# Combining attention branches: one broadcast multiply and one addition in place of four fused operations per head group

## The chip, the cores and the metric

One Trainium2 chip, one core of it. The metric is device time in microseconds (us) of one execution; each version is run several times and the median counts.

## What is computed

One decoder layer on 1024 tokens of width 1024, in float32. Attention has three families of heads side by side: 4 "nsa" heads, 8 sliding-window heads with sinks ("swa") and 4 stick-breaking heads ("sb"). Their outputs are normalised by family, concatenated and multiplied by an output matrix; a SwiGLU feed-forward block follows. The change touches the nsa family, whose output is a gated sum of three attentions over the same queries:

```python
def nsa_mixer(q, k_cmp, v_cmp, k_slc, v_slc, k_win, v_win, gate_logits, ...):
    kc, vc = nsa_compress(k_cmp, ...), nsa_compress(v_cmp, ...)
    o_cmp, o_slc = nsa_cmp_and_select(q, kc, vc, k_slc, v_slc, bias_tab)
    o_win = banded_attention(q, k_win, v_win, NSA_WINDOW, bias_tab)
    g = jax.nn.sigmoid(gate_logits)...          # one gate per token, branch and head
    return g[0] * o_cmp + g[1] * o_slc + g[2] * o_win
```

## The kernel before

The work is cut into tiles of 128 tokens, so there are 8 tiles (`n` = 0 to 7). A **job** is one kind of attention for one tile and four heads: 8 jobs "sb", 16 "swa", and then, for each tile, "win", "cmp" and "slc" of the nsa family, 24 jobs, which run in the trace from about 365 to 514 us.

A job goes through all engines. TensorE makes scores into PSUM (`scores`, lines 1042 to 1050). VectorE adds the bias and takes the row minimum (`logits`, 1452). ScalarE takes the exponential (`softmax`, 1247). TensorE transposes the weights block by block (`turn`, 1077). ScalarE or VectorE copies the block to SBUF (`keep`, lines 1277 and 1482). TensorE multiplies it with the values (`weigh`, 1097), 66 columns for each of four heads: 64 of output, and one of ones that gives the softmax denominator. All jobs accumulate in the same PSUM bank (`SUMS`, bank 7). So the first `weigh` of a job waits until the job before it is combined (`wait_combined`, semaphore `combined`).

`combine` (1491) runs on VectorE: it makes the coefficients from the denominators and the gates (two small instructions, 1505 and 1508) and applies them. For "win" and "swa" that is one multiplication of all 256 columns with the coefficients broadcast (1512). For "cmp" and "slc" it is four instructions, one for each head, that multiply 64 columns in PSUM and add them to `mix_n` in SBUF in the same pass (1518).

After "slc" the tile is normalised. ScalarE takes the squares (`squares`, 1297), VectorE scales their sum (`mean_squares`, 1524), POOL takes the root (866), VectorE multiplies (`norm_mix`, 1532), and TensorE transposes the result (`turn` of the family, 1066).

The order of instructions on each engine is not written by hand. `plan_attention` (254) is a list scheduler that runs when the kernel is built: each piece of work has an engine, a cost in ns, predecessors and an age, and the planner lets each engine take the piece that can start first, by age where several can. Its result is the order of the queues of TensorE, ScalarE, VectorE and SP (which issues the DMAs) for the whole of attention, about 125 to 519 us. Four other kinds of work are in that plan as well: `piece` (960), six products of 512 columns that are still left of the input projection and fill TensorE where nothing else is ready, up to about 365 us; `half_keep` (1178, 1364), which empties their one PSUM bank; `out_hi` and `out_lo` (1311, 1542), which split the output matrix into two parts, and `mix_hi` and `mix_lo` (1317, 1547), which do so for the first two tiles of the result; and `spread`, the DMAs (784) that lay out the queries of a group.

Behind attention lie the output product, the feed-forward block and the last normalisation (class `Finish`), which takes its roots on POOL (2652, 2656) with an exponent tile `mhalf` that it sets itself (2608).

Of the kernel before, what the change touches and what calls it, by code (L numbers as in the profile page):

```python
# [19 lines left out]
ALU = mybir.AluOpType  # L20
ACT = mybir.ActivationFunctionType

P = 128
# [230 lines left out]
def plan_attention(lay):  # L254
# [21 lines left out]
    for s in range(FIRST_PIECE, PIECES):  # L276
        h, n = s // 4, item_of(s)
        kind = T_TILES[h // 2][0]
        needs = [("cut_lo", n) if n >= FIRST_ITEMS else None]
        if s % 4 == 0 and h > FIRST_HALVES + 1:  # L280
            needs.append(("half_keep", h - 1))
        add(("piece", s), "pe", 6 * 226.5, needs, 1e4 + s)
        if s % 4 == 3 and h >= LAST_KEPT:
            add(("half_keep", h), "dve", dve(HALF), [("piece", s), ("half_scale", LAST_KEPT - 1)], -100)
        elif s % 4 == 3:
            add(("half_keep", h), "act", act(HALF), [("piece", s), ("half_lo", h - 10 if kind == "k" else 21) if h >= 20 else None], -100)
            add(("half_scale", h), "pool", 1650, [("half_keep", h)], -100)
# [19 lines left out]

    for j, job in enumerate(jobs):
# [60 lines left out]
        if job.kind == "sb":  # L369
            fresh = [("turn", lay.turn_at["sb", n - 2])] if n >= 2 else []  # L370
            add(("stick_combine", n), "act", act(256), [last] + fresh, age)
        else:
            fresh = [("turn", lay.turn_at[job.family, n - 2])] if n >= 2 else [("turn", lay.turn_at["sb", NT - 1])] if job.kind == "swa" else []
            extra = [("sink_exp", lay.j_swa[j])] if job.kind == "swa" else []
            add(("combine", m), "dve", {"swa": 900, "win": 650}.get(job.kind, 1100), [last] + fresh + extra, age)
        if job.kind in ("sb", "slc") or job.strip == 4:
            i, width = NT * FAMILIES.index(job.family) + n, FAMILY_WIDTH[job.family]
            age = 10.0 * j + 20
            add(("squares", i), "act", act(width, 250), [("stick_combine", n) if job.kind == "sb" else ("combine", m)], age)
# [86 lines left out]
def mixers(nc, core, x_rows, w_first, w_tiles, w_values, ln_pre, cmp, rel_bias, onehot, sinks, grp_g, w_out, ln_post, ln_ffn_pre, tables, keep):  # L466
# [15 lines left out]
    softmax_jobs = [j for j in range(lay.NJ) if jobs[j].kind != "sb"]  # L482
    NPHI = 8

    with ExitStack() as st:
# [96 lines left out]
        combined, stick_combined = sem("combined"), sem("stick_combined")  # L582
# [537 lines left out]
        def act_program(act, o):  # L1120
# [168 lines left out]
            def squares_(i):  # L1289
                family, n = FAMILIES[i // NT], i % NT  # L1290
                if family == "sb":
                    act.wait_ge(stick_combined, n + 1)
                else:
                    act.wait_ge(combined, 2 * n + 2 if family == "swa" else 2 * NT + 3 * n + 3)
                if i:
                    act.wait_ge(squares, i)
                act.activation(junk[:, 0:FAMILY_WIDTH[family]], mix_of(family, n), ACT.Square, accum_out=ss[:, i:i + 1]).then_inc(squares, 1)
# [27 lines left out]
        def dve_program(dve, o):  # L1325
# [165 lines left out]
            def combine(v):  # L1491
# [53 lines left out]
            def mix_lo(t):  # L1545
# [6 lines left out]
                    "combine": combine, "mean_squares": mean_squares, "norm_mix": norm_mix}  # L1552
# [78 lines left out]
def out_and_ffn(nc, core, x, x1, w_gate, w_up, w_pairs, act_pairs, keep, mem, fin):  # L1631
# [330 lines left out]
    def pool_program(pool):  # L1962
# [24 lines left out]
        fin.constants(pool)  # L1987
# [565 lines left out]
    o = {"w": w, "mH": mH, "mL": mL, "gpost": gpost, "gpre": gpre, "g_in": g_in, "wH_done": wH_done, "wL_done": wL_done,  # L2553
# [4 lines left out]
class Finish:  # L2558
# [3 lines left out]
    def __init__(self, core, stack, x1, ln_post, out, y_part, xt, gain, gained_last, junk):  # L2562
# [4 lines left out]
        self.ss, self.half, self.ms, self.rs, self.mhalf = sb("ss", [P, 2, NT]), sb("half", [P, NT]), sb("ms", [P, NT]), sb("rs", [P, NT]), sb("mhalf", [P, M_PAIRS])  # L2567
        self.x_in = [sem(f"x_in{t}") for t in range(4)]
        self.g_in, self.mhalf_set = sem("g_in"), sem("mhalf_set")
# [36 lines left out]

    def constants(self, pool):
        pool.memset(self.mhalf[:], -0.5).then_inc(self.mhalf_set, 1)
# [40 lines left out]
    def first_roots(self, pool):  # L2649
        pool.wait_ge(self.mhalf_set, 1)  # L2650
        pool.wait_ge(self.ms_done, 1)
        pool.tensor_tensor(self.rs[:, 0:M_PAIRS], self.ms[:, 0:M_PAIRS], self.mhalf[:], ALU.pow).then_inc(self.rs_done, 1)

    def root(self, pool, t):
        pool.wait_ge(self.late_ms, t - M_PAIRS + 1)
        pool.tensor_tensor(self.rs[:, t:t + 1], self.ms[:, t:t + 1], self.mhalf[:, 0:1], ALU.pow).then_inc(self.rs_done, 1)
# [28 lines left out]
def build_layer(nc, ins, out):  # L2685
# [7 lines left out]
    with ExitStack() as stack:  # L2693
# [17 lines left out]
        with ExitStack() as ffn:  # L2711
# [25 lines left out]
            with ExitStack() as early:  # L2737
# [5 lines left out]
                         (mem["xt_up"], mem["xt_sums"], mem["xt_spare"]), mem["last_gain"], mem["gained_last"], mem["last_junk"])  # L2743
# [95 lines left out]
```

## Time and profile before

| | us |
|---|---|
| median of 3 runs | 1252.41 |
| the three runs | 1250.11, 1252.41, 1258.15 |
| the profiled execution | 1252.77 |
| its span, first to last instruction | 1251.0 |
| busy: TensorE (PE) | 1217.7 |
| busy: TensorE weight loads (PEld) | 1042.2 |
| busy: VectorE (DVE) | 866.4 |
| busy: ScalarE (ACT) | 605.7 |
| busy: GpSimd (POOL) | 181.4 |

A profile tells when each instruction ran. TensorE has two rows, PE for products and PEld for the loads of the stationary operand, which overlap with them. An engine that idles is of interest only if the end of the program hangs on it. For that the profile gives the chain that ended last, and for each wait the instruction that ended it. "Granted clock" is the share of its full speed (2.4 GHz) that TensorE was given: 1.00, or 0.50 for 1.2 GHz.

### The profile page before, as it was taken

The numbers are of one execution on the slowest core, as the hardware profiler recorded it, in microseconds if no ns is written. First come the engines' busy times: TensorE is split into PE (matmuls) and PEld (weight loads), VectorE is DVE, ScalarE is ACT, GpSimd is POOL, SyncE is SP. The second block draws the span as 40 slices with busy tenths as digits, with TensorE's granted clock in tenths as the row PEclk, the third lists the DMA queues.
The fourth block names the chain that finished last, engine by engine and source line by source line (L and its number), as shares of the span: only waits on it lengthen the run. The fifth ranks groups of instructions, "written<-read, shape, count | busy, mean of one in ns | idle before, by whom it ended". The sixth has DMA issues, their size and how long they took to land.

```text
span 1251.0 us, 18763 instructions
## 1 busy us (share of the span) xinstructions
PE 1217.7 (97%) x6592; PEld 1042.2 (83%) x6592; DVE 866.4 (69%) x1641; ACT 605.7 (48%) x1167; POOL 181.4 (15%) x153
## 2 busy tenths in 40 slices
PE   9999999999999999999989999999999999999996
PEld 7898878888988999888878888888888888788885
DVE  6323788858878665355876657667666568897888
ACT  5432677657776566344653333333333345444343
POOL 5230111111000000011001112112122021000114
PEclk9999999999999999999999999999999999999998
DMA  6303511136842100222312232333332455743443
GB/s 234 120 1 119 118 37 49 35 110 158 182 121 77 26 18 18 68 101 100 119 42 100 94 125 67 103 127 103 108 105 72 144 193 195 259 156 115 151 169 135
DMA packets 66881, 136.93 MB, mean 109 GB/s; under 512 B 8503, under 2 KB 27199, under 8 KB 66788
## 3 DMA queue, kind: packets, MB, share of 16 engines
q1 hardware_dynamic: 66788, 135.74, 34.0%
q8 instruction: 53, 0.87, 0.3%
q14 instruction: 40, 0.33, 0.1%
HBM read 90.33 MB, written 28.60 MB: 95 GB/s over the span
## 4 chain that ended last, share of the span: by engine, by line
PE 79%; DVE 9%; issue 5%; ACT 3%; DMA 2%; SPq 1%; DVEq 0%; POOL 0%; ACTq 0%; POOLq 0%
PE ps L2506 32%; PE ps L2536 11%; PE ps L1097 7%; PE ps L2450 6%; PE ps L941 4%; PE ps L1077 4%; PE ps L886 3%; PE ps L960 3%; PE ps L1042 2%; PE ps L1050 2%; DVE ring L1468 2%; PE ps L975 1%; DMA m_qs<-m_qn 1%; DVE ring L1460 1%; DVE QT L2325 1%
## 5 line engine op out<-in xcount | busy, mean ns | idle before, releaser
L2506 PE MATMUL ps<-f_topH,f_W 128*128 128x512 f32 x704 | 221.0, 389 | 3.8 <-DVE f_W L2292 2.1
L2506 PEld LDWEIGHTS ps<-f_topH,f_W 128*128 128x128 f32 x704 | 132.1, 188 | 32.0 <-DVE f_W L2292 4.6
L2292 DVE TENSOR_TENSOR f_W<-f_scr,f_W 128x512 fp32r<-128x512 f32 (+1 forms) x128 | 89.9, 705 | 84.9 <-ACT f_W L2057 84.8
L2506 PE MATMUL ps<-f_topL,f_W 128*128 128x512 f32 x352 | 136.9, 389 | 0.0
L1097 PE MATMUL ps<-V,m_tw 128*128 128x66 f32 (+1 forms) x1056 | 129.2, 273 | 2.3 <-DVE m_mix_n L1518 2.2
L1097 PEld LDWEIGHTS ps<-V,m_tw 128*128 128x128 f32 x1056 | 126.3, 193 | 5.3 <-DVE m_mix_n L1518 4.3
L2536 PE MATMUL ps<-f_headH,f_W 128*128 128x512 f32 x408 | 128.0, 390 | 2.2 <-issue 1.5
L2506 PE MATMUL ps<-f_headH,f_W 128*128 128x512 f32 x352 | 114.7, 390 | 0.0
L2536 PEld LDWEIGHTS ps<-f_headH,f_W 128*128 128x128 f32 x408 | 76.6, 188 | 19.6 <-issue 2.7
L2057 ACT CAST f_W<-f_scr 128x512 fp32r<-128x512 f32 (+1 forms) x128 | 77.6, 610 | 24.6 <-PE ps L2536 15.2
L2292 DVE TENSOR_TENSOR f_W<-ring,f_W 128x512 fp32r<-128x512 f32 x60 | 59.6, 1006 | 33.4 <-ACT f_W L2057 33.3
L1277 ACT COPY m_tw<-ps 128x512 f32<-128x512 f32 (+1 forms) x101 | 56.5, 568 | 52.0 <-PE ps L1097 29.8
L2536 PE MATMUL ps<-f_headL,f_W 128*128 128x512 f32 x204 | 79.4, 389 | 0.0
L2506 PEld LDWEIGHTS ps<-f_topL,f_W 128*128 128x128 f32 x352 | 66.1, 188 | 13.7
L2506 PEld LDWEIGHTS ps<-f_headH,f_W 128*128 128x128 f32 x352 | 66.1, 188 | 13.6
L2506 PE MATMUL ps<-f_headL,f_W 128*128 128x512 f32 x176 | 68.5, 389 | 0.0
L960 PE MATMUL ps<-m_hH,m_wH 128*128 128x512 f32 x144 | 60.4, 419 | 4.9 <-ACT QT L1178 4.8
L2536 PE MATMUL ps<-f_b22H,f_W 128*128 128x512 f32 x208 | 65.1, 389 | 0.0
L2450 PE MATMUL ps<-o_w,o_mH 128*128 128x512 f32 x224 | 60.5, 392 | 0.0
L2506 PE MATMUL ps<-f_b22H,f_W 128*128 128x512 f32 x176 | 57.8, 389 | 0.0
L2325 DVE TENSOR_TENSOR QT<-ps,QT 128x512 f32<-128x512 f32 x68 | 46.7, 687 | 15.7 <-PE ps L2536 15.7
L1042 PE MATMUL ps<-m_KSa,m_qs 128*128 128x256 f32 (+7 forms) x168 | 55.0, 345 | 2.3 <-DVE m_rows_sb L1475 1.2
(279 smaller groups left out, 2660.4 us busy)
## 6 DMA issues: line engine op xcount, KB each, us to landing
act_pairs<-QT SPq DMA_DIRECT2D x77, 256.0 KB, 4.1
m_qs<-m_qn SPq DMA_DIRECT2D x128, 128.0 KB, 2.4
ring<-in_ffn_w_up SPq DMA_DIRECT2D x22, 512.0 KB, 3.7
f_stage<-act_pairs SPq DMA_DIRECT2D x40, 256.0 KB, 3.6
ring<-in_ffn_w_gate SPq DMA_DIRECT2D x19, 512.0 KB, 4.5
f_scr<-act_pairs SPq DMA_DIRECT2D x37, 256.0 KB, 3.1
ring<-in_ffn_w_down SPq DMA_DIRECT2D x11, 512.0 KB, 5.3
f_pair_up<-in_ffn_w_down SPq DMA_DIRECT2D x11, 512.0 KB, 6.6
```

What stands on the lines that cost most here:

```text
L941: ins = pe.matmul(ps[:, b + a, 0:VW_HALF], h[:, k, tok], wv[:, w, k, a * VW_HALF:(a + 1) * VW_HALF], start=(k == 0 and h is hH and w == 0) ...
L960: ins = pe.matmul(ps[:, bank, :], w[:, n % W_ITEMS, cols], a[:, k, hf * HALF:(hf + 1) * HALF], start=(k == 0 and w is wH and a is hH), sto ...
L1042: pe.matmul(out, q_hi_, k, start=True, stop=False)
L1077: ins = pe.transpose(ps[:, bank, i * P:(i + 1) * P], rows, ident[:])
L1097: ins = pe.matmul(ps[:, SUMS, wide * i:wide * (i + 1)], tw[:, t % W_SLOTS, P * i:P * i + P], v, start=(kb == 0 and i == 0), stop=(kb == jo ...
L1277: act.copy(out, src).then_inc(kept_by["act"], 1)
L2057: act.copy(slot_part(s, 0), source(s)).then_inc(hi_done, 1)
L2292: dve.tensor_tensor(slot_part(s, 1), source(s), slot_part(s, 0).bitcast(F32), ALU.subtract).then_inc(lo_done, 1)
L2325: dve.tensor_tensor(part, product_, part, ALU.add).then_inc(y_added, 1)
L2450: ins = pe.matmul(ps[:, 2 * (t % 2) + hf, :], m[:, t % 2, k, :], w[k][:, a, hf * HALF:(hf + 1) * HALF], start=(k == 0 and m is mH and a == ...
L2506: ins = pe.matmul(ps[:, bank, :], whole[:, w, cols], halves[h][:, k0 + k, col:col + HALF], start=(begins and k == 0 and w == 0 and h == 0) ...
L2536: ins = pe.matmul(ps[:, bank, :], whole[:, w, k * P:(k + 1) * P], block(n)[h], start=(begins and k == 0 and w == 0 and h == 0), stop=(k == ...
```

## The change

Three things change in the nsa family and its plan, and one at the end of the program.

1. For "cmp" and "slc", `combine` multiplies all four heads by one broadcast multiplication out of PSUM, as "win" did before, but into a spare tile in SBUF (`tmp`, 256 columns of it). `combined` is raised by that multiplication. A second step, `mix_add`, adds `tmp` to `mix_n`. It is a piece of work of its own in the plan, behind its `combine`; the next "cmp" or "slc" `combine` waits for it, as `tmp` is there once.
2. The squares of an nsa tile wait for `mix_add` of "slc" and no longer for `combined`.
3. Costs in the plan: `piece` 6 x 231 ns for 6 x 226.5; `combine` 800 ns for all kinds, before 900 (swa), 650 (win) and 1100 (cmp, slc); `mix_add` has the planner's cost of 256 columns on VectorE.
4. `Finish` uses the exponent tile that the output product's part has set already, in place of its own, whose memset goes.

```diff
-        add(("piece", s), "pe", 6 * 226.5, needs, 1e4 + s)
+        add(("piece", s), "pe", 6 * 231, needs, 1e4 + s)
...
-            add(("combine", m), "dve", {"swa": 900, "win": 650}.get(job.kind, 1100), [last] + fresh + extra, age)
+            two_step = job.kind in ("cmp", "slc")
+            added = [("mix_add", two_steps - 1)] if two_step and two_steps else []
+            add(("combine", m), "dve", 800, [last] + fresh + extra + added, age)
+            if two_step:
+                add(("mix_add", two_steps), "dve", dve(256), [("combine", m)], age + 0.5)
+                two_steps += 1
...
-                    act.wait_ge(combined, 2 * n + 2 if family == "swa" else 2 * NT + 3 * n + 3)
+                    if family == "swa":
+                        act.wait_ge(combined, 2 * n + 2)
+                    else:
+                        act.wait_ge(mix_added, 2 * n + 2)
...
                 if job.kind in ("swa", "win"):
-                    ins = dve.tensor_tensor(mix[:, job.mix_at:job.mix_at + 4 * HD].rearrange("p (h d) -> p h d", d=HD),
-                                            sums[:, :, 0:HD], coef[:, a].unsqueeze(2).broadcast_to([P, 4, HD]), ALU.mult)
+                    out = mix[:, job.mix_at:job.mix_at + 4 * HD]
                 else:
-                    dve.wait_ge(combined, v)
-                    for i in range(4):
-                        dst = mix[:, HD * i:HD * i + HD]
-                        ins = dve.scalar_tensor_tensor(out=dst, in0=sums[:, i, 0:HD], scalar=coef[:, a][:, i:i + 1], in1=dst,
-                                                       op0=ALU.mult, op1=ALU.add)
-                ins.then_inc(combined, 1)
+                    out = o["tmp"][:, 0:4 * HD]
+                    dve.wait_ge(piece_done, pieces(PIECES))
+                    if two_step_jobs.index(j):
+                        dve.wait_ge(mix_added, two_step_jobs.index(j))
+                dve.tensor_tensor(out.rearrange("p (h d) -> p h d", d=HD), sums[:, :, 0:HD],
+                                  coef[:, a].unsqueeze(2).broadcast_to([P, 4, HD]), ALU.mult).then_inc(combined, 1)
+
+            def mix_add(i):
+
+                j = two_step_jobs[i]
+                mix = mix_of("nsa", jobs[j].n)[:, 0:4 * HD]
+                dve.wait_ge(combined, j_sm[j] + 1)
+                if jobs[j].kind == "slc":
+                    dve.wait_ge(mix_added, i)
+                dve.tensor_tensor(mix, mix, o["tmp"][:, 0:4 * HD], ALU.add).then_inc(mix_added, 1)
...
-        fin.constants(pool)
...
-    def constants(self, pool):
-        pool.memset(self.mhalf[:], -0.5).then_inc(self.mhalf_set, 1)
...
-        pool.wait_ge(self.mhalf_set, 1)
```

## Rows read from the trace of the kernel before

**Rows 1.** The page of the profile: span, then busy time, share, instructions
```profile
span 1251.0 us, 18763 instructions
PE 1217.7 (97%) x6592; PEld 1042.2 (83%) x6592; DVE 866.4 (69%) x1641; ACT 605.7 (48%) x1167; POOL 181.4 (15%) x153
...
PE 79%; DVE 9%; issue 5%; ACT 3%; DMA 2%; SPq 1%; DVEq 0%; POOL 0%; ACTq 0%; POOLq 0%
```

**Rows 2.** Stretches: length, busy time (instructions) by engine, granted clock, DMA share, GB/s
```profile
140.00:290.00 150.00, 142.37 (x882) 123.65 (x881) 121.21 (x175) 105.42 (x216) 24.05 (x20) 0.99 0.25 68
290.00:365.00 75.00, 74.28 (x580) 70.38 (x579) 59.19 (x232) 49.76 (x129) 6.62 (x10) 1.00 0.62 146
365.00:405.00 40.00, 35.84 (x249) 31.96 (x248) 36.80 (x151) 31.02 (x68) 3.08 (x4) 0.96 0.36 107
405.00:510.00 105.00, 104.49 (x805) 97.25 (x804) 63.16 (x251) 59.64 (x105) 2.17 (x4) 0.98 0.09 21
```

**Rows 3.** By line: ns min/median/max, first and last start; who waited (us, times)
```profile
L1518 DVE SCALAR_TENSOR_TENSOR m_mix_n<-ps,m_coef,m_mix_n x64: 273/276/285, 372.0 to 513.9; 128x64 f32<-128x64 f32 x64
...
  PEld ps L1097: 4.3, 8
...
  PE ps L1097: 2.2, 3
...
L1512 DVE TENSOR_TENSOR m_mix_n<-ps,m_coef x8: 424/424/425, 367.5 to 499.0; 128x256 f32<-128x256 f32 x8
```

**Rows 4.** Timeline (start, us, engine, line, count), two stretches of the nsa jobs
```profile
375.87 0.97 PEld L1097 LDWEIGHTS ps<-V,m_tw 128*128 128x128 f32 x8 [0.53 <-DVE m_mix_n L1518]
...
400.54 0.86 DVE L1518 SCALAR_TENSOR_TENSOR m_mix_n<-ps,m_coef,m_mix_n 128x64 f32<-128x64 f32 x4
401.31 0.28 DVE L1452 CUSTOM_DVE_ANT_0 m_rows_slc<-ps,m_strip_full,m_neg 128x64 f32<-128x64 f32 x1
...
401.45 1.76 PEld L1097 LDWEIGHTS ps<-V,m_tw 128*128 128x128 f32 x8 [1.76 <-DVE m_mix_n L1518]
401.45 1.95 PE L1097 MATMUL ps<-V,m_tw 128*128 128x66 f32 x8 [1.52 <-DVE m_mix_n L1518]
```

**Rows 5.** Timeline, VectorE: instructions of 256 columns, each with its follower
```profile
377.77 0.42 DVE L1421 TENSOR_TENSOR m_qn<-QT,m_qn 128x256 fp32r<-128x256 f32 x1
378.10 0.48 DVE L1532 SCALAR_TENSOR_TENSOR m_mix_n<-m_mix_n,m_rs,m_g_sb 128x256 f32<-128x256 f32 x1
...
380.14 0.42 DVE L1512 TENSOR_TENSOR m_mix_n<-ps,m_coef 128x256 f32<-128x256 f32 x1
...
380.49 0.68 DVE L1482 COPY m_tw<-ps 128x512 f32<-128x512 f32 x1
```

**Rows 6.** Stretches at the low and at the full clock, columns of rows 2
```profile
401.45:408.30 6.85, 6.85 (x28) 6.85 (x29) 4.21 (x19) 4.07 (x7) 0.54 (x1) 0.50 0.50 145
230.94:234.20 3.26, 3.26 (x8) 2.59 (x9) 3.26 (x4) 0.15 (x1) 1.53 (x1) 0.50 0.00 0
...
630.00:632.00 2.00, 0.49 (x2) 0.45 (x3) 2.00 (x4) 2.00 (x5) 0.00 (x0) 1.00 0.00 0
```

**Rows 7.** Timeline, TensorE: the first products behind two other stops
```profile
230.94 0.77 PE L960 MATMUL ps<-m_hH,m_wH 128*128 128x512 f32 x1 [2.29 <-ACT QT L1178]
...
631.51 0.50 PE L2506 MATMUL ps<-f_topH,f_W 128*128 128x512 f32 x1 [2.13 <-DVE f_W L2292]
```

**Rows 8.** Timeline, 389 to 392 us: a root on POOL beside VectorE
```profile
389.45 1.22 DVE L1547 TENSOR_TENSOR o_mL<-QT,o_mH 128x1024 fp32r<-128x1024 f32 x1
389.61 1.46 POOL L866 TENSOR_TENSOR m_rs<-m_ms,m_mhalf 128x1 f32<-128x1 f32 x1 [11.83 <-DVE m_ms L1524]
...
391.80 0.41 PE L1066 MATMUL ps<-ident,m_mix_n 128*128 128x128 f32 x2 [0.27 <-DVE m_mix_n L1532]
```

**Rows 9.** By line: the memset of the last part
```profile
L2608 POOL MEMSET e_mhalf<- x1: 93/93/93, 1035.8 to 1035.8; 128x4 f32 x1
```

More of the change, by code:

```diff
@@ L306, in plan_attention @@
     add(("strip", 4), "dma", 3000, [("norm_mix", NT - 1)], -100)
+    two_steps = 0
     for j, job in enumerate(jobs):
@@ L378, in plan_attention @@
             age = 10.0 * j + 20
-            add(("squares", i), "act", act(width, 250), [("stick_combine", n) if job.kind == "sb" else ("combine", m)], age)
+            add(("squares", i), "act", act(width, 250), [("stick_combine", n) if job.kind == "sb" else ("mix_add", two_steps - 1) if job.kind == "slc" else ("combine", m)], age)
             add(("mean_squares", i), "dve", 100, [("squares", i)], age)
@@ L482, in mixers @@
     softmax_jobs = [j for j in range(lay.NJ) if jobs[j].kind != "sb"]
+    two_step_jobs = [j for j in range(lay.NJ) if jobs[j].kind in ("cmp", "slc")]
     NPHI = 8
@@ L581, in mixers @@
         kept_by = {"act": sem("turn_kept_by_act"), "dve": sem("turn_kept_by_dve")}
-        combined, stick_combined = sem("combined"), sem("stick_combined")
+        combined, stick_combined, mix_added = sem("combined"), sem("stick_combined"), sem("mix_added")
         squares, ms_ready, rs_ready, normed = sem("squares"), sem("ms_ready"), sem("rs_ready"), sem("normed")
@@ L1551, in dve_program @@
                     "stick_scan": stick_scan, "stick_sub": stick_sub, "keep": keep_turn, "sink_arg": sink_arg_,
-                    "combine": combine, "mean_squares": mean_squares, "norm_mix": norm_mix}
+                    "combine": combine, "mix_add": mix_add, "mean_squares": mean_squares, "norm_mix": norm_mix}
             for what, arg in plan["dve"]:
@@ L2551, in pe_program @@
                 product(s)
-    o = {"w": w, "mH": mH, "mL": mL, "gpost": gpost, "gpre": gpre, "g_in": g_in, "wH_done": wH_done, "wL_done": wL_done,
+    o = {"w": w, "tmp": tmp, "mH": mH, "mL": mL, "gpost": gpost, "gpre": gpre, "g_in": g_in, "wH_done": wH_done, "wL_done": wL_done,
          "mH_done": mH_done, "mL_done": mL_done, "y_done": y_done}
@@ L2558, with __init__ @@
 class Finish:
-    def __init__(self, core, stack, x1, ln_post, out, y_part, xt, gain, gained_last, junk):
+    def __init__(self, core, stack, x1, ln_post, out, y_part, xt, gain, gained_last, junk, mhalf):
         sb = lambda n, s, d=F32: core.sb("e_" + n, s, d, stack)
@@ L2566, in __init__ @@
         self.y, self.xt, self.gain, self.gained_last, self.junk = y_part, xt, gain, gained_last, junk
-        self.ss, self.half, self.ms, self.rs, self.mhalf = sb("ss", [P, 2, NT]), sb("half", [P, NT]), sb("ms", [P, NT]), sb("rs", [P, NT]), sb("mhalf", [P, M_PAIRS])
+        self.ss, self.half, self.ms, self.rs = sb("ss", [P, 2, NT]), sb("half", [P, NT]), sb("ms", [P, NT]), sb("rs", [P, NT])
         self.x_in = [sem(f"x_in{t}") for t in range(4)]
-        self.g_in, self.mhalf_set = sem("g_in"), sem("mhalf_set")
+        self.g_in, self.mhalf = sem("g_in"), mhalf
         self.squares, self.gained, self.late_gained, self.late_ms = sem("squares"), sem("gained"), sem("late_gained"), sem("late_ms")
@@ L2649, in first_roots @@
     def first_roots(self, pool):
-        pool.wait_ge(self.mhalf_set, 1)
         pool.wait_ge(self.ms_done, 1)
-        pool.tensor_tensor(self.rs[:, 0:M_PAIRS], self.ms[:, 0:M_PAIRS], self.mhalf[:], ALU.pow).then_inc(self.rs_done, 1)
+        pool.tensor_tensor(self.rs[:, 0:M_PAIRS], self.ms[:, 0:M_PAIRS], self.mhalf[:].broadcast_to([P, M_PAIRS]), ALU.pow).then_inc(self.rs_done, 1)
     def root(self, pool, t):
         pool.wait_ge(self.late_ms, t - M_PAIRS + 1)
-        pool.tensor_tensor(self.rs[:, t:t + 1], self.ms[:, t:t + 1], self.mhalf[:, 0:1], ALU.pow).then_inc(self.rs_done, 1)
+        pool.tensor_tensor(self.rs[:, t:t + 1], self.ms[:, t:t + 1], self.mhalf[:], ALU.pow).then_inc(self.rs_done, 1)
     def wait_gained(self, dve, t):
@@ L2742, in build_layer @@
             fin = Finish(core, ffn, x1, ins["ln_ffn_post"], out, keep["QT"][:].rearrange("p k (h q) -> p (k h) q", h=2),
-                         (mem["xt_up"], mem["xt_sums"], mem["xt_spare"]), mem["last_gain"], mem["gained_last"], mem["last_junk"])
+                         (mem["xt_up"], mem["xt_sums"], mem["xt_spare"]), mem["last_gain"], mem["gained_last"], mem["last_junk"], mem["mhalf"])
             o, ffn_programs = out_and_ffn(nc, core, x, x1, ins["ffn_w_gate"], ins["ffn_w_up"], ins["ffn_w_down"], act_pairs, keep, mem, fin)
```

## The prediction

> **What bounds the kernel now.** I read the page first: TensorE is busy for 1217.7 of 1251.0 us, and the chain that ended last runs on it for 79% [rows 1]. VectorE, where the change is made, is at 69%, so time taken off VectorE counts only where TensorE waits for it. The table of stretches says where that is [rows 2]. From 405 to 510 us, where nine of the sixteen changed combines run, TensorE idles 0.5 us of 105. From 365 to 405 us, where six of them run, it idles 4.2 us of 40, and VectorE is busy for 36.8: there VectorE sets the pace. From 140 to 290 us TensorE idles 7.6 us of 150, and no changed instruction lies there, only a plan made anew. Behind attention the output product and the feed-forward block are dense and bound by TensorE, so what attention saves arrives at the end whole.
>
> The waits name the place itself: weight loads of `weigh` (1097) waited 4.3 us in 8 places for the four fused operations of line 1518, and products 2.2 us in 3 of them [rows 3]. The longest is at 401.45: 1.52 us without a product [rows 4]. Behind it the granted clock is 0.50 for 6.85 us [rows 6].
>
> **The release of the sums' bank.** Before, the bank is free when the fourth fused operation ends: 276 ns each, but they overlap, and the four take 0.86 us from start to end [rows 3, 4]. After, one broadcast multiplication releases it; "win" has the same instruction with the same operands but for the place of its output, 424 ns [rows 3]. The coefficients before it do not change. The release comes 0.86 - 0.42 = 0.44 us earlier, sixteen times. That is worth nothing where TensorE has other work in its queue. The bounds: TensorE's own stops of 2.2 us are 1.52 and two that share the 0.7 left. The first gives 0.44 back and the others at most 0.7, together 1.1 us. If the weight loads set the pace (66 columns are short beside a load), the 1.76 us stop gives 0.44 and the seven others at most 4.3 - 1.76 = 2.5, together 2.9 us [rows 3, 4]. For the low end, some of it passes to the next wait, VectorE's pace. I take 1.5 us, near the lower of the two, since from 405 us on TensorE is full.
>
> **VectorE's own time.** Before, the instruction behind the four starts 401.31 - 400.54 = 0.77 us after the first [rows 4]. After: the broadcast multiplication holds the engine for 380.49 - 380.14 = 0.35 us. The addition (256 columns, both inputs and output in SBUF) is not in the trace; its nearest row is the subtraction of line 1421, which holds it for 378.10 - 377.77 = 0.33 us [rows 5]. With other work between them the pair costs 0.68. With the addition directly behind, it must wait for the multiplication's end, 0.42 + 0.33 = 0.75 and some hundredths for the semaphore. So VectorE gains 0.1 us a time or nothing: at most 0.6 us over the six in the stretch that it paces, which I count as zero. What is cut is the delay of the release, not the engine's load.
>
> The Trainium skill ("VectorE: DVE Perf Modes", section "The DRAIN you can't avoid") says that the next operation does not start until the pipeline of the one before has emptied, though one that is not held starts earlier. By its first clause the four would hold the engine for 4 x 0.276 = 1.1 us and the new pair for 0.85, a gain of 0.25 x 16 = 4 us of VectorE; the rows have 0.77, so this trace goes by the second clause and the gain is near zero.
>
> **The clock.** The stop of 1.52 us ends at half clock [rows 4, 6]. It would be 1.08 us after the change. A stop's length alone does not decide: 2.29 us at 230.94 was followed by the low clock, 2.13 us at 631.51 was not [rows 6, 7]. What differs is what went before: around 631 us the products are long and dense, from 365 to 405 us there is a row of shorter stops, and the change shortens several of them. I hold it for a little more likely than not that this fall goes. Its price: the eight loads of one weigh step take 1.76 us there and 0.97 us at full clock [rows 4], so at least 0.8 us comes back; at most it is half of 6.85, 3.4 us, if nothing but TensorE's clock set the pace. Logits on VectorE follow those scores at their own pace, so I take 2.0 us.
>
> **The later users of the sum.** The nsa squares now wait for multiplication and addition, 0.42 + 0.42 us and a semaphore, against 0.86: no change, if the addition follows at once. In the plan it is a piece of work of its own, ready 130 ns after `combine`, so VectorE may take another piece first. For "cmp" that costs nothing, nobody but VectorE waits for it. For "slc", squares, mean, root, norm_mix and TensorE's transpose stand behind it in that order. TensorE has already waited 0.27 us for a norm_mix at 391.80 [rows 8]. That is a rival below. I price it at zero in the sum, as TensorE's transpose is elsewhere queued behind other products.
>
> **The addition beside POOL.** Before, the fused operations read one tensor from PSUM; the addition reads two from SBUF. At 389.61 a root on POOL took 1.46 us beside a VectorE operation with two SBUF inputs that ran from 389.45 for 1.22 [rows 8]. POOL does little from 365 to 510 us (5.3 us busy [rows 2]), and the root of a tile comes after its own additions; a meeting costs about one addition, 0.42 us. I price it at zero, at most 8 x 0.42 = 3.4 if each root met one and nothing hid it.
>
> The Trainium skill ("SBUF — State Buffer", section "SBUF: two separate sides") says that a VectorE operation with two SBUF inputs and a GpSimd operation that reads SBUF exclude each other for a whole instruction. This speaks against the change; the 1.46 us root agrees with it. By it the sum stays within the bound just given.
>
> **The rest.** Costs in the plan are no work; they only reorder queues from about 125 us on, the DMA issues on SP too. `piece` at 231 for 226.5 moves TensorE's filler by 27 ns apiece, under 2 us over the 68 left, enough to change neighbours. This can go either way and is priced in the rivals. The memset that goes took 93 ns on POOL at 1035.8, far ahead of its user [rows 9]: zero.
>
> **The sum.** 1.5 + 2.0 = 3.5 us off the profiled execution of 1252.77 (span 1251.0 and 1.8 around it) gives 1249.3; that execution is 0.4 above the median, so 1248.9, say 1249.
>
> **The rivals.**
> 1. *Only the release counts; the low clock stays, or comes at another stop.* For it: the stop at 401.45 is still over 1 us. 1252.4 - 1.5 = 1251.
> 2. *No net gain.* TensorE waits for logits in place of the combine, since VectorE is as busy as before, or a stop of attention's first part grows by what is won. 1252.4.
> 3. *The new order helps the first part.* There 7.6 us idle and the low clock behind 230.94 (3.26 us at half, 1.6 lost [rows 6]) are at stake, 9.2 together. If half of it goes, 4.6 more than forecast: 1244.3. Against it: these stops end on ScalarE's emptying of the pieces' bank, which the change leaves alone.
> 4. *Slower: the addition comes late.* VectorE takes one long piece (1.22 us [rows 8]) between "slc" multiplication and addition, and norm_mix and TensorE's transpose shift by it. If four tiles have no slack, 4.9 us less the 1.5 won: 1255.8. It decides from two tiles on (2.4 us); at six it is 7.3 - 1.5, 1258. Against it: waits for norm_mix before are only some tenths.
>
> **How the numbers follow.** Forecast 1249: 0.36. Rival 1: 0.20. Rival 2: 0.16. Rival 3: 0.16. Rival 4: 0.12. The range, 1243 to 1256, takes in rivals 1 and 2, rival 3 at 1244.3 with a little below it, and rival 4 at 1255.8 but not its dearer form; the three runs of before lie 2.3 below to 5.7 above their median, so a median can miss its case by some 2 us. That leaves out under 0.2. One per cent is 12.5 us, about what a measurement of this kernel can tell from no change. Faster than 1239.9 needs all of the first part's 9.2 us besides the 3.5: 0.05. Slower than 1264.9 needs all eight tiles late by 1.2 us, 9.8, and more low clock on top: 0.03. Within 1%: 0.92.
>
> **What would show it.** Line 1512 with 40 instructions of 424 ns; an addition of about 420 ns, 16 times; line 1518 gone. The first weigh behind a "cmp" or "slc" starts about 0.5 us after the multiplication starts. Waits for the combine fall from 4.3 us to under 2. TensorE idles under 3 us in the nsa jobs' first 40 us, with a granted clock of 1.00. Feed-forward and end keep their lengths. The forecast is wrong if the low clock stays, if TensorE's wait for norm_mix grows beyond 1 us, or if the idle time from 140 to 290 us moves by more than 3 us.

## The result and the profile after

| | before | after |
|---|---|---|
| median of 10 runs each, us | 1251.88 (1248.59 to 1258.15) | 1257.98 (1252.98 to 1261.50) |
| span of the profiled execution | 1251.0 | 1259.7 |

The ratio is 1.0043, 95% interval 1.0022 to 1.0064. The medians lie 6.1 us apart; by the ratio the change costs 5.4 us (2.8 to 8.0). It is slower by less than the one per cent that the prediction called "within", but it went the other way than forecast (1249) and left the range (1243 to 1256) at the top.

Below, "x us by the ratio" means (ratio - 1) x 1252. Each experiment was run 5 to 12 times beside 11 to 35 runs of the kernel before on the same chip, and its ratio is to those.

The page of the kernel after (span; busy time, share, instructions; shares of the chain that ended last), against [rows 1]:

```profile
span 1259.7 us, 18737 instructions
PE 1223.8 (97%) x6592; PEld 1047.1 (83%) x6592; DVE 862.1 (68%) x1608; ACT 604.7 (48%) x1168; POOL 179.4 (14%) x152
...
PE 83%; DVE 7%; issue 4%; ACT 4%; DMA 1%; SPq 1%; POOL 0%; DVEq 0%; ACTq 0%; POOLq 0%
```

VectorE has 4.3 us less to do, TensorE is busy for 6.1 us more with the same 6592 products: part of them ran at half clock. The stretches of [rows 2], in the kernel after (columns as there):

```profile
140.00:290.00 150.00, 139.82 (x866) 121.38 (x864) 116.30 (x165) 102.58 (x208) 24.02 (x20) 0.99 0.23 63
290.00:365.00 75.00, 74.19 (x569) 69.19 (x570) 62.92 (x236) 49.37 (x134) 6.84 (x11) 1.00 0.66 156
365.00:405.00 40.00, 34.68 (x231) 31.66 (x230) 31.66 (x124) 28.94 (x65) 1.62 (x3) 0.91 0.42 118
405.00:510.00 105.00, 104.47 (x782) 95.64 (x781) 67.18 (x253) 61.66 (x113) 2.70 (x5) 0.97 0.08 21
```

TensorE idles 10.2 us of the first stretch (7.6 before), and in the third it idles 5.3 us at a granted clock of 0.91 (4.2 us at 0.96 before). VectorE has only 31.7 us of work there against 36.8: it no longer sets the pace, and TensorE still waits more.

To compare kernels whose starts differ, I cut each span at four events: the first `piece`, the last weights of "sb", the first gate coefficient of "nsa", the first output product.

| us | front | sb | swa | nsa | output and the rest | span |
|---|---|---|---|---|---|---|
| before | 119.3 | 144.8 | 102.9 | 154.3 | 729.6 | 1251.0 |
| after | 122.3 | 147.1 | 104.4 | 156.6 | 729.3 | 1259.7 |

The front is ahead of everything that the change touches and took from 118.3 to 122.4 us over seventeen profiles, without regard to the kernel, so its 3.0 us are no work of the change (the last section shows what they hang on). The other 5.7 us are three stages, 2.3 + 1.5 + 2.2, less 0.3. Only the last of the three holds a changed instruction. Each row is one execution, and that of the kernel after, 1261.50 us, is the slowest of its ten, so I read from the stages where time was lost and from the ratios how much.

The new instructions, by line (ns min/median/max, first and last start, who waited for it), against [rows 3]:

```profile
L1528 DVE TENSOR_TENSOR o_tmp<-ps,m_coef x16: 423/424/425, 378.1 to 522.2; 128x256 f32<-128x256 f32 x16
...
  PEld ps L1104: 5.2, 6
  PE ps L1104: 2.7, 1
...
L1538 DVE TENSOR_TENSOR m_mix_n<-m_mix_n,o_tmp x16: 414/419/427, 378.8 to 522.7; 128x256 f32<-128x256 f32 x16
...
  ACT m_junk L1307: 0.4, 2
```

They cost what was forecast, 424 ns and 419 ns. TensorE waits for them in fewer places, 6 for 8, but for 5.2 us where it was 4.3, and one stop of 2.7 us holds more than half. This is it, in the timeline of the kernel after:

```profile
378.13 0.42 DVE L1528 TENSOR_TENSOR o_tmp<-ps,m_coef 128x256 f32<-128x256 f32 x1
...
378.61 1.11 PE L1104 MATMUL ps<-V,m_tw 128*128 128x66 f32 x8
...
378.81 0.42 DVE L1538 TENSOR_TENSOR m_mix_n<-m_mix_n,o_tmp 128x256 f32<-128x256 f32 x1
...
380.65 0.40 ACT L1248 CAST m_qn<-QT 128x256 fp32r<-128x256 f32 x1 [1.17 <-DMA m_qs<-m_qn]
...
381.09 0.42 DVE L1431 TENSOR_TENSOR m_qn<-QT,m_qn 128x256 fp32r<-128x256 f32 x1 [1.86 <-ACT m_qn L1248]
381.43 1.22 DVE L1560 TENSOR_TENSOR o_w<-ring,o_w 128x1024 fp32r<-128x1024 f32 x1
...
382.57 0.15 DVE L1515 SCALAR_TENSOR_TENSOR m_coef<-ps,gate 128x4 f32<-128x4 f32 x1
...
382.97 0.42 DVE L1528 TENSOR_TENSOR o_tmp<-ps,m_coef 128x256 f32<-128x256 f32 x1
...
383.45 0.97 PE L1104 MATMUL ps<-V,m_tw 128*128 128x66 f32 x5 [2.67 <-DVE o_tmp L1528]
```

The first pair works as meant: multiplication at 378.13, next `weigh` 0.48 us later, addition behind it. The eight products at 378.61 are the next job's `weigh` ("slc" of tile 0) and end at 379.72, yet its coefficients start at 382.57. VectorE's queue holds two other pieces ahead of them. `query_lo` (1431) stood 1.86 us on ScalarE's `query_hi` (1248), and that on the DMAs that lay out the queries; then came `out_lo` (1560) with 1.22 us. In the order of before, this `combine` stands ahead of both. The DMAs themselves are not late. SP's queue issued them at 373.63 and before at 368.04, but the nsa stage also starts later, at 373.84 for 367.06: against its start they come 1.2 us earlier. What changed is the place of the pieces that wait for them. First after, then before (start, us of the issues, line, count):

```profile
373.63 3.09 SPq L791 DMA_DIRECT2D m_qs<-m_qn  x4
```

```profile
368.04 2.86 SPq L784 DMA_DIRECT2D m_qs<-m_qn  x4
```

Behind the stop the clock falls, and a second time near 482, with no stop over 0.3 us in the 25 us ahead of it (stretches of the kernel after, columns as in [rows 2]):

```profile
383.00:390.00 7.00, 6.55 (x26) 6.21 (x27) 5.54 (x23) 3.52 (x10) 0.54 (x1) 0.56 0.28 75
482.00:489.00 7.00, 7.00 (x37) 6.90 (x37) 2.75 (x15) 2.77 (x8) 0.00 (x0) 0.56 0.00 0
```

### The profile page after: what moved, and what is told of

Read it like the earlier page. It is cut to its first block, busy times and chain, and to the rows that moved or that the text cites. A ratio compares the mean times of both kernels' runs of the same rounds, so it can differ in the third digit from the quotient of the medians.

```text
span 1259.7 us, 18737 instructions
## 1 busy us (share of the span) xinstructions
PE 1223.8 (97%) x6592; PEld 1047.1 (83%) x6592; DVE 862.1 (68%) x1608; ACT 604.7 (48%) x1168; POOL 179.4 (14%) x152
## 4 chain that ended last, share of the span: by engine, by line
PE 83%; DVE 7%; issue 4%; ACT 4%; DMA 1%; SPq 1%; POOL 0%; DVEq 0%; ACTq 0%; POOLq 0%
PE ps L2523 32%; PE ps L2553 12%; PE ps L1104 8%; PE ps L2467 6%; PE ps L967 4%; PE ps L1084 4%; PE ps L948 4%; PE ps L893 4%; PE ps L1049 3%; PE ps L1057 2%; PE ps L982 1%; PE ps L1115 1%; DVE m_rows_sb L1485 1%; DMA m_qs<-m_qn 1%; DVE QT L2342 1%
## 5 line engine op out<-in xcount | busy, mean ns | idle before, releaser
L967 PE MATMUL ps<-m_hH,m_wL 128*128 128x512 f32 x144 | 57.4, 398 | 0.0
```

The source lines that it names most:

```text
L967: ins = pe.matmul(ps[:, bank, :], w[:, n % W_ITEMS, cols], a[:, k, hf * HALF:(hf + 1) * HALF], start=(k == 0 and w is wH and a is hH), sto ...
```

## The experiments

**The instructions or the order.** The change has two halves that can be had apart: what VectorE executes, and the plan's inputs, which give every engine another order. The planner's code, run for both kernels, gives queues of the same 596 pieces of work on TensorE, of which at least 105 have to be moved to turn one order into the other; of SP's 52 it is 6. On ScalarE and VectorE 41 copies (`keep`) also change the engine. Kernel e1 has the new instructions in exactly the old order, with the addition directly behind its multiplication; e2 has the four fused instructions in the new order.

```diff
# e1, against the kernel after
-        add(("piece", s), "pe", 6 * 231, needs, 1e4 + s)
+        add(("piece", s), "pe", 6 * 226.5, needs, 1e4 + s)
-            add(("combine", m), "dve", 800, [last] + fresh + extra + added, age)
+            add(("combine", m), "dve", {"swa": 900, "win": 650}.get(job.kind, 1100), [last] + fresh + extra, age)
...  (the addition's piece goes, and the squares follow `combine`)
                                   coef[:, a].unsqueeze(2).broadcast_to([P, 4, HD]), ALU.mult).then_inc(combined, 1)
+                if job.kind in ("cmp", "slc"):
+                    mix_add(two_step_jobs.index(j))
# e2, against the kernel after: combine() and the squares' wait are those of before, and
...
             def mix_add(i):
+                pass
```

> The two new instructions in the order that the kernel before has on every engine (the addition directly behind its multiplication, all costs in the plan as before). Theory O (the loss is the new order, the new instructions gain a little): 1249 to 1252, ratio to before 0.997 to 1.000, stops of TensorE and the clock from 140 to 365 us as in before. Rival I (the new instructions themselves cost: the wait between multiplication and addition, or POOL beside the addition): 1255 to 1258, ratio 1.003 to 1.005, with longer waits for the combine in the nsa jobs.

> The four fused operations in the new order of every engine (the addition's place in the plan does nothing). Theory O: 1257 to 1260, as the changed kernel or a little above it, ratio to before 1.004 to 1.007. Rival I: 1250 to 1253, ratio 0.999 to 1.001.

| | median us | ratio (95%) | by the ratio |
|---|---|---|---|
| e1 new instructions, old order | 1251.56 | 0.9995 (0.9984 to 1.0006) | -0.6 |
| e2 old instructions, new order | 1262.08 | 1.0079 (1.0064 to 1.0095) | +9.9 |

Theory O of the expectations says that the order costs it, rival I that the new instructions do. The loss is the order's: e1 came as O expected, and e2 even above its 1257 to 1260. With the old instructions the new order costs 9.9 us; the new ones take back some 4.5 of them (e2 to after; the two intervals together leave about 3 either way). In the old order they give 0.6 with zero inside the interval. The stop of [rows 4] at 401.45 (1.52 us, then half clock) looks like this in e1:

```profile
403.88 1.11 PE L1100 MATMUL ps<-V,m_tw 128*128 128x66 f32 x8 [1.24 <-DVE o_tmp L1524]
```

shorter by 0.28 us, and eight products take 1.11 us where they took 1.95: full clock. The nsa stage took 152.0 us against 154.3. The 2.67 us stop of the new order stands in e2 as well, with the old instructions, at 2.97 us:

```profile
382.98 1.34 PE L1104 MATMUL ps<-V,m_tw 128*128 128x66 f32 x5 [2.97 <-DVE m_mix_n L1528]
```

**Which of the costs.** Three edits feed the planner: `piece` 226.5 to 231, `combine` to 800 for all kinds, and the addition as a piece of work of its own.

```diff
# e3: before, with 6 * 231 for piece        # e8: before, with 800 for every combine
# e4: after, with 6 * 226.5 for piece       # e7: after, with all old costs; the addition keeps its piece
# e12: e7, with 800 for "cmp" and "slc" alone
```

> The kernel before with one number changed: 231 for 226.5 ns in the planned cost of a piece. Theory O splits here. If the pieces' new order is the larger part (the changed kernel's stretch up to the last stick-breaking row was 2.3 us longer in its profile), 1254 to 1256, ratio 1.002 to 1.004. If the order behind it is (combine costs, the addition as work of its own), 1252, ratio 0.999 to 1.001. Rival I: 1252.

> The changed kernel with the planned cost of a piece put back to 226.5 ns. Counterpart of the run before: if the pieces' order is the larger part, 1253 to 1255, ratio to before 1.001 to 1.003; if the rest of the plan is, 1257 to 1258, ratio 1.004 to 1.005. Rival I: 1257 to 1258.

> The changed kernel with all costs in the plan as before (226.5; 900, 650 and 1100), the addition still a piece of work of its own. The planner then puts the combine of tile 0's cmp ahead of query_lo by itself. Theory Q: 1250 to 1252, ratio 0.998 to 1.001. Rival P, that the addition as a piece of its own makes a worse order: 1254 to 1257.

> The kernel before, with only the planned cost of every combine changed to 800 ns. The planner then puts out_lo, not query_lo, ahead of the combine of tile 0's cmp. Theory Q: no 2.7 us stop, 1251 to 1254, ratio 1.000 to 1.002. Rival P, that the combine's wrong cost for four long operations (they take 1.27 us with the coefficients) spoils the order by itself: 1256 and above.

> The changed kernel with piece 226.5, swa 900 and win 650 as before, and 800 ns only for cmp and slc; the addition a piece of its own. The order up to the nsa jobs is that of the kernel before, and query_lo stands where it did. Theory Q2: 1249 to 1252, ratio 0.997 to 1.000. Rival P: 1254 to 1256.

| | piece | combine swa / win / cmp, slc | addition's own piece | median | ratio (95%) | by the ratio |
|---|---|---|---|---|---|---|
| e7 | 226.5 | 900 / 650 / 1100 | yes | 1252.07 | 0.9996 (0.9986 to 1.0005) | -0.5 |
| e12 | 226.5 | 900 / 650 / 800 | yes | 1251.90 | 0.9999 (0.9985 to 1.0013) | -0.1 |
| e8 | 226.5 | 800 / 800 / 800 | no | 1253.09 | 1.0017 (1.0003 to 1.0030) | +2.1 |
| e4 | 226.5 | 800 / 800 / 800 | yes | 1255.57 | 1.0026 (1.0013 to 1.0039) | +3.3 |
| e3 | 231 | 900 / 650 / 1100 | no | 1257.11 | 1.0041 (1.0029 to 1.0053) | +5.1 |
| after | 231 | 800 / 800 / 800 | yes | 1257.98 | 1.0043 (1.0022 to 1.0064) | +5.4 |

By their ratios e7, e8 and e12 came as theory Q of the expectations (Q2 in e12) had it, a misplaced `combine` that is taken up below, and e4 as theory O. The addition's own piece and the lower cost of "cmp" and "slc" lose nothing; what e4 has beyond e12 is the 800 for "swa" and "win". The largest single edit is 4.5 ns in the planned duration of a product: 5.1 us, with no instruction changed. It came out above the 1254 to 1256 that was expected of it. The effects do not add up (5.1 and 3.3 would be 8.4): each set of costs is simply another order.

The stages say where it acts. The sb stage took 143.7 to 144.8 us in all ten profiles with 226.5 (mean 144.2), and 146.7 to 147.7 in all seven with 231 (mean 147.3): 3.1 us, without overlap. The swa stage took 102.2 to 103.7 us in five profiles with the old cost for it, and 104.0 to 105.1 in nine with 800, 1.1 us more (e13 to e15, below, whose moves reach into it, are left out). That is not all of e3's 5.1 us: in its one profile the sb stage is 2.9 us longer than in before and the swa stage 0.7, but the nsa stage 1.0 and the rest 0.4 shorter. Where the remainder lies stays open. e3's first stretch looks like that of after, with TensorE idle for 10.9 us:

```profile
140.00:290.00 150.00, 139.15 (x862) 120.92 (x860) 115.67 (x164) 101.94 (x206) 23.33 (x20) 0.99 0.24 63
```

TensorE stops for over half a microsecond five times in the sb stage of before, 6.3 us in all, and seven times in e3, 9.7 us. Most of it ends on `half_keep`, ScalarE's emptying of the pieces' bank. These are the rows of who waited for that line (us, times), first in before, then in e3; in after TensorE's wait is the same 7.2 us in 5 places:

```profile
L1178 ACT ACTIVATE QT<-ps x14: 577/593/629, 49.9 to 320.1; 128x512 f32<-128x512 f32 x14
...
  PE ps L960: 4.8, 4
```

```profile
L1178 ACT ACTIVATE QT<-ps x14: 578/593/630, 50.1 to 326.2; 128x512 f32<-128x512 f32 x14
...
  PE ps L960: 7.2, 5
```

The longest of these in the kernel after, first TensorE's timeline, then ScalarE's:

```profile
209.08 0.39 PE L967 MATMUL ps<-m_hH,m_wL 128*128 128x512 f32 x1
212.08 0.47 PE L967 MATMUL ps<-m_hH,m_wH 128*128 128x512 f32 x1 [2.61 <-ACT QT L1185]
```

```profile
209.21 0.85 ACT L1266 ACTIVATE ring<-ps 128x512 f32<-128x512 f32 x2
210.09 0.84 ACT L1273 ACTIVATE ring<-ring 128x768 f32<-128x768 f32 x1
210.84 0.60 ACT L1169 CAST m_wH<-ring 128x512 fp32r<-128x512 f32 x1
211.35 0.59 ACT L1185 ACTIVATE QT<-ps 128x512 f32<-128x512 f32 x1
```

The piece's last product started at 209.08, ScalarE is at work without a gap, and `half_keep` (1185) stands behind four other instructions (1266 twice, 1273, 1169). TensorE has the next piece in front and nothing to overtake it with. A stop of this kind was there before as well (2.29 us at 230.94, [rows 7]); a new order adds some.

**The stop at 383.** Two theories: (A) it is the one misplaced `combine`, and putting it right brings the nsa stage back; (B) the time is lost because the clock falls behind the stop. e5 moves `combine` 18 ahead of `query_lo` and `out_lo` on VectorE and nothing else; e6 does so with 226.5. In the expectations A is theory Q and B is theory C. They call this `combine` "cmp"; it is that of tile 0's "slc". e9 leaves the order alone and has TensorE multiply through the stop: 16 products of 256 columns into a free bank that nobody reads, besides all the kernel's work.

```diff
# e5 and e6, behind the plan
+    ahead("dve", ("combine", 18), ("query_lo", 29))
# e9, in the queue of TensorE ahead of the weigh that stood
+                if t == turn0[27]:
+                    wait_kept(pe, lay.same_bank_before[88])
+                    for _ in range(FILL):
+                        pe.matmul(ps[:, lay.bank_of_turn[88], 0:256], identr[:], KS[0][:, 0, 0:256], start=True, stop=True)
```

> The changed kernel with one piece of work moved in VectorE's order: the combine of tile 0's cmp stands ahead of the splitting of the next queries (query_lo) and of out_lo, where it stood behind both. Theory Q (in the changed order that combine is queued behind query_lo, which waits for a DMA; TensorE stops 2.7 us and the low clock follows): the stop and that low clock go, 1252 to 1255, ratio to before 1.000 to 1.002. Rival P (the loss behind the stick-breaking jobs is spread over many moved pieces, this stop would only move on): 1256 to 1258, ratio 1.003 to 1.005.

> Both undone: a piece costs 226.5 ns in the plan, and the combine of tile 0's cmp stands ahead of query_lo. Theory Q: the changed kernel's loss is these two together, 1249 to 1252, ratio 0.998 to 1.000. Rival P: 1254 to 1256, ratio 1.002 to 1.003, as without the move.

> The changed kernel with 16 products of 256 columns put in front of the first weigh of tile 1's win, where TensorE stopped 2.7 us at 380.8 in the changed kernel's profile. They go to a bank that the next transpose writes over; nothing reads them. They shorten no wait and fill about 1.9 us of the stop. Theory C (much of what the stop costs is the low clock behind it): no low clock from 383 to 390, 1254 to 1256, ratio 1.001 to 1.003. Rival D (the stop itself and the order cost it, the clock little): 1257 to 1259, ratio 1.004 to 1.006.

| | median | ratio (95%) | by the ratio | nsa stage | half of its time at the low clock |
|---|---|---|---|---|---|
| after | 1257.98 | 1.0043 (1.0022 to 1.0064) | +5.4 | 156.6 | 6.8 |
| e5 | 1256.51 | 1.0036 (1.0022 to 1.0049) | +4.5 | 155.4 | 5.1 |
| e6 | 1253.33 | 1.0014 (1.0002 to 1.0026) | +1.8 | 153.1 | 3.4 |
| e9 | 1255.17 | 1.0022 (1.0006 to 1.0037) | +2.8 | 151.2 | 0 |

Theory A fell. In e5 the wait changes its name and keeps its length; the logits now stand behind the same DMA and `out_lo`:

```profile
383.69 0.47 PE L1056 MATMUL ps<-m_KSa,m_qs 128*128 128x448 f32 x1 [2.86 <-DVE m_neg L1469]
```

In e9 the added products fill the hole and the rest of the wait is short (timeline of TensorE, and two of its stretches):

```profile
376.67 2.15 PE L1099 MATMUL ps<-m_KSa,m_identr 128*128 128x256 f32 x16
379.61 1.11 PE L1109 MATMUL ps<-V,m_tw 128*128 128x66 f32 x8 [0.78 <-DVE o_tmp L1533]
```

```profile
381.00:390.00 9.00, 7.36 (x54) 6.52 (x53) 8.79 (x35) 6.67 (x16) 0.54 (x1) 1.00 0.58 176
480.00:490.00 10.00, 10.00 (x77) 9.32 (x76) 5.74 (x19) 4.88 (x9) 0.00 (x0) 1.00 0.01 2
```

Its nsa stage has no low clock at all, though the kernel does more. The filling can account for the first of the two stretches that are gone. The second, near 482, lies 100 us behind it in the same order, and the longest stop ahead of it is 0.26 us in both kernels: why it is gone is not shown, and it may be chance. By the ratios that is worth 2.6 us, but the two intervals overlap, and the profiled execution is one of e9's fastest (1252.28), so its 5.4 us less in the stage are more than the kernel's share. What supports theory B over all profiles: the five nsa stages with no low clock (e1, e3, e7, e8, e9) took 151.2 to 153.4 us, whatever their order; eight others (before, after, e2, e4, e5, e6, e10, e11) lost 3.4 to 6.8 us to the half clock, by half its length, and took 153.1 to 159.6. e12, with 1.7, took 151.9. That is a correlation over single profiles, not a proof. e6 undoes both the cost of `piece` and the misplaced `combine`, and still took 1.8 us more than before, between what theory and rival expected.

**The pieces in front.** e10 and e11 delay the query pieces and `out_lo` instead; e13 to e15 put the long pieces (`out_lo` 1 to 3, `mix_lo` 0 and 1) behind the first three tiles. In SP's queue they leave the loads of the output matrix's last blocks, each of which waits for one of these `out_lo`, behind the spread of group 28 but ahead of that of group 29. e13 does it to after, e14 to e12, e15 to before.

```diff
# e10 (after) and e11 (with 226.5)
+    place("act", ("query_hi", 29), ("softmax", 88))
+    place("dve", ("query_lo", 29), ("out_lo", 2))
+    place("dve", ("out_lo", 1), ("out_lo", 2))
# e13, in short
+    place("dve", ("query_lo", 29), ("norm_mix", 16))
+    place("dve", ("out_lo", 1), ("logits", 118))
...
+    place("dve", ("mix_lo", 1), ("logits", 133))
+    place("dma", ("out", 5), ("spread", 29))
...
```

> The changed kernel with the splitting of the queries of group 29, two tiles ahead of their use, moved later on both engines: query_hi behind the copies of turns 86 and 87 on ScalarE, query_lo and one out_lo behind the logits of tile 1 on VectorE, about where the kernel before has them. Moving the combine ahead of them alone left a stop of 2.86 us for logits. Theory Q2 (both engines stand still for query_hi's DMA, and everything behind it is late): no stop over 1.3 us from 375 to 390, 1253 to 1256, ratio 1.001 to 1.003. Rival P (the stop moves on again): 1257 to 1258, ratio 1.004 to 1.005.

> The same move with the planned cost of a piece back at 226.5 ns. Theory Q2: the whole loss is undone and the new instructions' gain shows, 1249 to 1252, ratio 0.997 to 1.000. Rival P: 1253 to 1256, ratio 1.001 to 1.003.

> The changed kernel's order, but VectorE's long pieces that nobody needs yet (three out_lo and two mix_lo of 1.2 us) and the early query_hi and query_lo moved out of the first tiles' nsa jobs, to tile 3, where VectorE has room; SP's loads that wait for them moved behind the next spread. Theory L (each stop comes from such a piece that the planner put ahead of a combine or of logits; moving one leaves the next): no stop over 1.5 us in the nsa jobs and no low clock from 375 to 400, 1254 to 1256, ratio 1.001 to 1.003, the rest being the earlier part's order. Rival P (VectorE's load sets the pace there whatever the order): 1257 to 1258, ratio 1.004.

> New instructions, the addition a piece of its own, planned costs 226.5, 900 and 650 as before and 800 only for cmp and slc, with the same long pieces moved to tile 3. Theory L: faster than both kernels, 1247 to 1250, ratio 0.995 to 0.998. Rival P: 1251 to 1253, ratio 0.999 to 1.001, as without the move.

> The kernel before, four fused operations, with the same long pieces moved to tile 3. Theory L: 1249 to 1251, ratio 0.997 to 0.999, so the move alone pays, and the new instructions, by the run above, 1 to 2 us more. Rival P: 1252 to 1253.

| | median | ratio (95%) | by the ratio |
|---|---|---|---|
| e10 | 1257.41 | 1.0031 (1.0016 to 1.0046) | +3.9 |
| e11 | 1254.16 | 1.0014 (0.9999 to 1.0029) | +1.8 |
| e13 | 1268.98 | 1.0136 (1.0119 to 1.0154) | +17.0 |
| e14 | 1259.68 | 1.0071 (1.0052 to 1.0089) | +8.9 |
| e15 | 1258.84 | 1.0057 (1.0040 to 1.0074) | +7.1 |

By their medians e10 and e11 came as rival P expected, that the stop moves on (e10's ratio lies between the two). In e10 the `combine` of "win" then stands behind two `out_lo`, and TensorE stops 2.79 us at 386.80. e13 shows in part that the long pieces slow the first tiles: the ninth combine of the nsa jobs comes 29.3 us after the first, 34.4 in after, and up to tile 3 no stop over 1.3 us is left (e15 30.6, before 33.1; but e14 32.9, e12 32.6). Then, in tile 3, this follows (e13, timeline of TensorE):

```profile
424.58 1.12 PE L1100 MATMUL ps<-ident,m_rows_slc 128*128 128x128 f32 x4 [5.66 <-ACT m_tw L1300]
```

That stop and the half clock behind it cost more than was won, and all three kernels lie above what either expectation allowed. The timelines show what it hangs on, first the two query pieces on ScalarE and VectorE, then SP's issues, and last what SP waited for from 365 to 430 us (us in total, times, longest):

```profile
423.42 0.41 ACT L1264 CAST m_qn<-QT 128x256 fp32r<-128x256 f32 x1 [6.13 <-DMA m_qs<-m_qn]
...
423.86 0.43 DVE L1447 TENSOR_TENSOR m_qn<-QT,m_qn 128x256 fp32r<-128x256 f32 x1 [6.45 <-ACT m_qn L1264]
```

```profile
416.81 2.56 SPq L807 DMA_DIRECT2D m_qs<-m_qn  x4
...
SPq L837 <- DVE o_w L1576: 30.1, 3, 25.4
```

SP stood 25.4 us on a moved `out_lo`, and issued the spread of group 29 (the DMAs at 416.81) directly behind the third load, at 416.38, with no other wait. ScalarE and VectorE then both stood over 6 us on that spread. e14 and e15 have the same waits (5.1 and 6.6 us on ScalarE). So the stop is not the long pieces' own 1.2 us each: by these profiles, the moves held up SP's queue. Whether the pieces fit in tile 3 when the loads are put behind the spread of group 29 too was not tried. No kernel here beats the one before by more than its interval.

## Why the prediction was wrong, point by point

- **What bounds the kernel**: right. Behind attention 729.6 us became 729.3, so what attention lost came out whole.
- **The release, 1.5 us**: the mechanism is right, the next `weigh` starts 0.48 us after the multiplication. Its worth in the old order, with the clock together, is 0.6 us measured (-0.8 to 2.0): the 3.5 forecast lie outside, so the gain was set too high even without the new order. At the stop of 401.45 it gave 0.28 us where the step had 0.44; where the rest went was not traced.
- **VectorE's own time, zero**: right. In e1 the multiplication starts at 403.40 and the instruction behind the addition at 404.20, so the pair holds the engine for 0.80 us where the four held it for 0.77. Busy time fell by 2.9 us of 866 in e1 and by 4.3 in after, and TensorE did not profit where it waited for a DMA.
- **The clock, 2.0 us**: the fall behind that stop is gone in e1. But no low clock came in the nsa stage of e3 and e8 either, which have the old four instructions: another order does as much, or chance. The step took the long and dense products around 631 us as the reason why the clock stayed up there; the same stop, behind the same instructions, was followed by the low clock in 11 of the 17 profiles (last section). In the new order the premise, that the stops there get shorter, was false: one of 2.67 us came, and two stretches at the low clock for one.
- **The later users, the addition late (rival 4)**: not what happened, although its 1255.8 is the nearest number. The additions never idled ahead, ScalarE waited for them 0.4 us in all, and in after TensorE's transpose never waited for an nsa `norm_mix`. In e1, the old order, it did once, for 1.17 us at 394.64, where before waited 0.27: part of what the new instructions won may have gone there.
- **POOL, the memset**: zero, as taken. The eight nsa roots took 0.54 us each in after, where one took 1.46 before, so none was held up beside an addition; POOL was busy for 2.0 us less.
- **"The rest. Costs in the plan are no work; they only reorder queues"**: this is the step that failed. The sum had zero for it, and only rival 3 had a number, with the opposite sign: the stops of the first part would shrink from 7.6 us. They grew to 10.2. Alone, the cost of `piece` is 5.1 us; all the new order with the old instructions is 9.9. The step said itself that 27 ns apiece was "enough to change neighbours" and that it "can go either way", and then gave the losing way no more than rival 2, where the first part loses what is won (1252.4). Had it mirrored rival 3 (4.6 us lost), that would have been 1253.5 with the gains and 1257.0 without them.
- **What would show it**: 40 multiplications of 424 ns, 16 additions of 419 ns, line 1518 gone, all as written. The waits for the combine were to fall under 2 us and rose from 4.3 to 5.2; TensorE was to idle under 3 us from 365 to 405 at clock 1.00 and idled 5.3 at 0.91. For 140 to 290 us I had set 3 us as the sign of error; 2.6 came, and were half the loss.

Three things stay open. Which of the pieces' new neighbours makes the sb stage 3.1 us longer was not tried one by one. Of e3's 5.1 us the stages of its profile show only part. And the nsa stage's loss could not be split for good between the order and the clock: e9 points to the clock, with overlapping intervals.

## What to carry to other kernels

When a list scheduler writes the queues, a changed cost is a changed program: time the new instructions in the old order and the old instructions in the new one before judging either. A more accurate cost gives another order, not a better one; keep the old number, or try several. And look for what stands ahead of the operation that frees a shared buffer: a piece that waits for a DMA, or a long piece of low priority, delays it by more than a faster release can win, and moving one such piece handed the wait to the next in e5 and e10. Where pieces are moved by hand, look at every queue that waits for them, the one that issues the DMAs above all: the longest stop of e13 came from there.

## What the runs showed of the hardware

**The low clock is not decided by the length of a stop.** With 226.5 for `piece`, this part of the order is that of before. A stop of 2.26 to 2.29 us near 231 us was followed by half clock in before, e1, e4, e7, e11, e12 and e14, and by full clock in e6, e8 and e15. First before at the place, then e8 (timelines of TensorE):

```profile
231.93 0.63 PE L960 MATMUL ps<-m_hH,m_wL 128*128 128x512 f32 x1
232.36 0.63 PE L960 MATMUL ps<-m_hH,m_wH 128*128 128x512 f32 x1
```

```profile
229.87 0.47 PE L960 MATMUL ps<-m_hH,m_wH 128*128 128x512 f32 x1 [2.29 <-ACT QT L1178]
```

A second case is the stop of 2.12 to 2.13 us in the feed-forward block, at 631.51 in [rows 7], behind instructions that no kernel here changes. It is in all 17 profiles. In six (before, after, e2, e5, e6, e9) the clock stayed at 1.00, in the other eleven it fell to half. Here is e11, 29 us of dense products ahead of the stop, then the stop, then the stretch behind it:

```profile
600.00:629.00 29.00, 29.00 (x137) 23.99 (x135) 26.87 (x38) 19.09 (x28) 1.84 (x2) 1.00 0.26 91
...
631.27 0.50 PE L2532 MATMUL ps<-f_topH,f_W 128*128 128x512 f32 x1 [2.13 <-DVE f_W L2318]
...
631.50:634.50 3.00, 3.00 (x10) 2.39 (x10) 2.72 (x5) 1.82 (x4) 0.00 (x0) 0.68 0.03 5
```

Before has 1.00 in the last stretch, with the same 29.00 us busy in the first. So neither the stop's length nor the products ahead of it decide here; what does is not shown. And in after the fall near 482 us has no stop over 0.3 us ahead; what ran there were scores of 64 columns and `weigh` products of 66. The Trainium skill ("TensorE: Matmul & The Clock Gate", section "Part 1: The HAM clock gate") says that how busy the engine has been recently sets which of the two levels is granted. A fall without a stop agrees with that; no run here shows which activity counts, and it does not tell the eleven profiles from the six. Some microseconds of difference between executions of one kernel can come from this alone: two nsa falls are worth up to 6.8 us in the profile of after.

**The front varies by itself.** The same instructions ahead of attention took from 118.3 to 122.4 us. It goes with the granted clock of the first 118 us: 1.00 in six profiles, with fronts of 118.3 to 119.3 us (before is one), 0.99 in four, 120.4 to 121.6, and 0.97 in seven, 121.9 to 122.4 (after is one). Two single profiles can differ by 4 us before the first changed instruction, where 6.1 us were to be explained; cutting the span into stages took it out.
